# A forgetting-attention bias added by matmul instead of by rows read back from memory

## What is computed

```python
def fox_prompt(q, k, v, logf):
    ft = jnp.swapaxes(jnp.cumsum(logf, axis=1), 1, 2)
    for blk in range(s_len // Q_BLOCK):          # 2 blocks of 128 queries
        q0 = blk * Q_BLOCK
        kend = q0 + Q_BLOCK
        sc = jnp.einsum('bqhd,bkhd->bhqk', q[:, q0:kend], k[:, :kend]) * scale
        bias = ft[:, :, q0:kend, None] - ft[:, :, None, :kend]
        mask = jnp.arange(kend)[None, :] <= (q0 + jnp.arange(Q_BLOCK))[:, None]
        p = jax.nn.softmax(jnp.where(mask, sc + bias, -jnp.inf), axis=-1)
        ...
```

## Time and profile before

| | us |
|---|---|
| median of 3 runs | 1481.11 |
| lowest, highest | 1472.64, 1483.24 |
| time of the profiled execution | 1481.11 |
| its span, from first to last instruction | 1479.1 |

### The profile page before, as it was taken

The page is one execution under the profiler, slowest core; times in us unless marked ns, Lnnn a source line. Parts: engine busy times, 40 slices in busy tenths (PEclk is TensorE's granted clock), DMA queues, the critical chain, the costliest instruction groups (busy, mean ns, idle before and its releaser), DMA issues.

```text
span 1479.1 us, 15869 instructions
## 1 busy us (share of the span) xinstructions
PE 1383.4 (94%) x6315; PEld 630.3 (43%) x6315; DVE 343.9 (23%) x699; ACT 231.9 (16%) x461; POOL 25.5 (2%) x55
## 2 busy tenths in 40 slices
PE   6899899999978999999999999999999999999996
PEld 2555536666446434434334344333343333433332
DVE  3441322434243211101201121021011110120113
ACT  2011410433243211101101011011010010110102
POOL 1100000001000100000000000000000000000000
PEclk9799989999987799999999999999999999999998
DMA  8655347443145679999999999999999999999992
GB/s 292 207 199 182 139 170 257 138 163 108 71 171 187 279 284 419 429 428 426 430 425 428 427 421 427 428 427 427 422 427 428 428 418 408 427 428 427 427 429 107
DMA packets 72476, 486.83 MB, mean 329 GB/s; under 512 B 10349, under 2 KB 15205, under 8 KB 47828
## 3 DMA queue, kind: packets, MB, share of 16 engines
q1 hardware_dynamic: 70724, 480.85, 79.4%
q0 software_dynamic: 1680, 4.91, 1.0%
HBM read 481.63 MB, written 4.12 MB: 328 GB/s over the span
## 4 chain that ended last, share of the span: by engine, by line
PE 76%; DMA 17%; DVE 2%; issue 2%; ACT 2%; SPq 1%; DVEq 0%; ACTq 0%; PEldq 0%
PE bank L1726 35%; DMA ring<-in_w_gate_up_dram 16%; PE bank L1373 9%; PE bank L1691 5%; PE bank L1400 4%; PE bank L1265 4%; PE bank L1714 3%; PE bank L1692 3%; PE bank L1560 2%; PE bank L1356 2%; PE bank L1517 1%; PE bank L1368 1%; PE bank L1355 1%; PE bank L1628 1%; PE bank L1646 1%
## 5 line engine op out<-in xcount | busy, mean ns | idle before, releaser
L1726 PE MATMUL bank<-ring,work 128*64 128x512 f32 x2048 | 457.2, 600 | 16.7 <-issue 10.8
L1726 PEld LDWEIGHTS bank<-ring,work 128*64 128x64 f32 x2048 | 161.1, 138 | 291.0 <-issue 290.8
L1726 PE MATMUL bank<-ring,hT 128*64 128x512 f32 x1024 | 233.3, 603 | 16.6 <-DMA ring<-in_w_gate_up_dram 16.6
L1242 DVE TENSOR_TENSOR gbT<-gbT,bank 128x512 f32<-128x512 f32 x85 | 58.4, 688 | 452.8 <-PE bank L1714 392.2
L1373 PE MATMUL bank<-hT,ring 128*128 128x320 f32 x512 | 143.4, 440 | 5.6 <-DVEq L805 4.9
L1726 PEld LDWEIGHTS bank<-ring,hT 128*64 128x64 f32 x1024 | 77.0, 138 | 161.5 <-issue 161.5
L1373 PEld LDWEIGHTS bank<-hT,ring 128*128 128x128 f32 x512 | 97.7, 193 | 53.5 <-issue 7.0
L1211 DVE TENSOR_SCALAR work<-bank 128x512 f32<-128x512 f32 x32 | 22.0, 686 | 322.8 <-PE bank L1726 322.8
L1400 PE MATMUL bank<-hT,ring 128*128 128x320 f32 x256 | 72.4, 436 | 0.0
L1691 PE MATMUL bank<-qT,tok 128*128 128x256 f32 x256 | 72.4, 405 | 0.0
L707 ACT ACTIVATE work<-bank 128x320 f32<-128x320 f32 x16 | 7.0, 438 | 408.4 <-PE bank L1265 408.4
(11 more groups left out here) (334 smaller groups left out, 894.2 us busy)
## 6 DMA issues: line engine op xcount, KB each, us to landing
ring<-in_w_gate_up_dram SPq DMA_DIRECT2D x128, 2048.0 KB, 14.8
ring<-in_w_down_dram SPq DMA_DIRECT2D x64, 2048.0 KB, 17.0
ring<-in_w_ada_dram SPq DMA_DIRECT2D x12, 2048.0 KB, 8.1
ring<-in_w_in_dram SPq DMA_DIRECT2D x12, 2048.0 KB, 9.8
ring<-in_cache_k_dram SPq DMA_DIRECT2D x16, 512.0 KB, 6.1
ring<-in_cache_v_dram SPq DMA_DIRECT2D x16, 512.0 KB, 4.5
ring<-in_w_out_dram SPq DMA_DIRECT2D x2, 2048.0 KB, 7.9
out_dram<-tok POOLq DMA_DIRECT2D x2, 1024.0 KB, 5.2
```

What stands on the lines that cost most here:

```text
L1242: TTo(piece(gbf, n), piece(gbf, n), B[6 + n % 2][:, :], ALU.add).then_inc(s["scatter_read"], 1)
L1726: last = mm(bank[CAP * x:CAP * x + CAP, :], lhsT[:, CAP * x:CAP * x + CAP], rhs(x), start=start, stop=stop)
```

## The change

The bias and the mask no longer meet in `biasF`. The write to and the six reads from `bias_rows`, `masked`, and the semaphores `bias_out`, `bias_in` and `bias_made` are gone. DVE adds the mask itself to the scores at L917. PE adds the bias row: after each two scores matmuls, which now leave the sum open (`stop=False`), it adds two matmuls of 16 rows, whose weights are one column of the identity, repeated 128 times, and whose moving operand is `Fp`. A one in row h of the weights picks row h of `Fp` for all 128 queries. For a pair of heads these are two of 128 columns and two of 256. `scores_ps` is raised by the last of a head's matmuls. PE waits for `F_made` ahead of `scores(0)`. On SyncE's queue chunks 7 to 21 stand together, and the wait for `rg_free` stands ahead of the first cached keys.

```diff
-            for c in range(7, 20):
+            for c in range(7, 22):
                 chunk(c)
-            eng.wait_ge(s["F_made"], 1)
-            eng.dma_start(bias_d, Fp).then_inc(s["bias_out"], 16)
-            chunk(20)
-            eng.wait_ge(s["rg_free"], 1)
-            eng.wait_ge(s["bias_out"], 16)
-            bias_rows(0, 8)
-            chunk(21)
...
             chunk(22)
-            eng.wait_ge(s["scores_read"], 4)
-            bias_rows(8, 12)
             chunk(23)
-            eng.wait_ge(s["scores_read"], 8)
-            eng.wait_ge(s["bias_made"], 2)
-            bias_rows(12, 16)
+            eng.wait_ge(s["rg_free"], 1)
             keys_in(0)
...
-            def masked(a, z):
-                eng.wait_ge(s["bias_in"], 32 * (1, 2, 3)[(z - 8) // 4])
-                v = biasF[:, a % 8:a % 8 + z - a, :].rearrange("p s (t n) -> p s t n", t=3)
-                for t in (0, 2):
-                    link.later(TTo(v[:, :, t, :], v[:, :, t, :], mask[:, 0:128].unsqueeze(1).to_broadcast([128, z - a, 128]), ALU.add))
-                eng.wait_ge(s["chain_dve"], link.n)
-                eng.sem_inc(s["bias_made"], 1)
-
...
-                TTo(P, B[h % 4][:, 0:384], biasF[:, h % 8, :], ALU.add).then_inc(s["scores_read"], 1)
+                TTo(P, B[h % 4][:, 0:384], mask, ALU.add).then_inc(s["scores_read"], 1)
...
-                        last = mm(B[2 * (p % 2) + o][:, c:c + n], qT[d, p, q:q + 128], kT[d, p, 0:n], start=True, stop=True)
+                        mm(B[2 * (p % 2) + o][:, c:c + n], qT[d, p, q:q + 128], kT[d, p, 0:n], start=True, stop=False)
+                    for o in range(2):
+                        row = ident[0:H, 2 * p + o:2 * p + o + 1].to_broadcast([H, 128])
+                        last = mm(B[2 * (p % 2) + o][:, c:c + n], row, Fp[:, 0:n], start=False, stop=True)
                         if c:
                             last.then_inc(s["scores_ps"], 1)
...
+            eng.wait_ge(s["F_made"], 1)
             scores(0)
             scores(1)
```

More of the change, by code:

```diff
@@ L126, in hybrid_layer @@
         U = Uf.rearrange("p (t c) -> p t c", t=NT)
-        biasF = work[:, 0:3072].rearrange("p (s n) -> p s n", s=8)
         Ssb = work[:, 3072:4608].rearrange("p (s n) -> p s n", s=4)
@@ L251, in hybrid_layer @@
             den_made mult_made st_made rg_done F_made
-            bias_out bias_in bias_made scores_ps scores_read negmax_made exp_done probs_made PT_ps PT_ev py_ps py_read
+            scores_ps scores_read negmax_made exp_done probs_made PT_ps PT_ev py_ps py_read
             qbd_zero qbd_made KT_ps KT_ev sscores_ps sscores_read snegmax_made sexp_done sprobs_made
@@ L295, in hybrid_layer @@
         G_K, G_LF, G_V, G_ST, G_CF = 0, 6, 7, 13, 15
-        bias_d = nc.dram_tensor("bias_rows", (H, SP_), f32, kind="Internal").ap()
         block = ctx.enter_context(nc.Block())
@@ L341, in chunk @@
                 eng.dma_start(wstage[c % 3], CHUNKS[c]).then_inc(chunk_in[c % 3], 16)
[L343 to L347, removed]
             for c in range(7):
@@ L938, in gated @@
                 link(STT(v, v, 1.0, windows(U, S0, DS)[:, t, :, :], ALU.add, ALU.mult))
-            masked(0, 8)
             for h in range(4):
@@ L945, in _ @@
                 head_norm(2 * p + 1)
-                if p in (2, 4):
-                    masked(4 * p // 2 + 4, 4 * p // 2 + 8)
                 if p + 2 < NT:
```

## The result

| | before | changed |
|---|---|---|
| median, us | 1480.14 (1472.64 to 1483.24, 4 runs) | 1499.64 (1498.5 to 1501.39, 4 runs) |
| profiled execution: time, span | 1481.11, 1479.1 | 1496.86, 1495.1 |

The changed kernel is slower: the ratio to the kernel before is 1.015 (95% interval 1.0126 to 1.0174), 19.5 us between the medians. A ratio here is not the quotient of two medians, which would be 1.013; a ratio of 1.015 stands for 22 us. I had forecast 11.9 us, and within 1% as the likeliest class.

A forecast was written before the change was run, and what follows sets the result against it. PE was taken to bound the prompt's attention, with shifts there reaching the end. Added matmuls of 12.6 us less a vanished wait of 0.7 gave 11.9 us, on 1481.1 us a forecast of 1493.0 us, range 1483 to 1502.

The forecast's parts named there:

- within 1%: Whole kernel's time: a change of less than one per cent, 14.8 us, either way; chance 0.67.
- That PE bounds the stretch, and that a shift there reaches the end whole: Prompt's attention, 263.8 to 360.2 us: PE busy 94.46 of 96.40 us; any shift before 518 us moves the end equally.
- DVE, DMA and queue parts at 0: Removed additions of 5.0 us on DVE, about 3 MB of bias rows and queue waits: counted as 0 gain.
- 2 us earlier and not 4: SyncE's queue: first cached keys issued some 4 us earlier than at 295.93, with no effect.
- The wait at 270.63 gone: PE's wait of 0.73 us for L927, first turned probabilities of head 0, disappears: -0.7 us.
- The added matmuls at 1.58 us a pair: Scores in the prompt's attention: 2 x 0.25 + 2 x 0.54 us a pair, 12.6 us for eight pairs.
- rival A: Scores blocks: three extra changes of shape a pair at 0.30 us each, 16.8 us, 1498 us; chance 0.19.
- The clock: Prompt's attention, 263.8 to 360.2 us: granted clock 1.00 in the profile; the sum had no term for a fall there.
- Rival B: From 410 to 520 us: shifted clock falls give back half of 24 us lost, 1481 us or less; chance 0.09.
- Rival D: Scores blocks: the two heads' additions share the array, 6.3 less 0.7 is 5.6 us, 1487 us; chance 0.09.

The follow-up runs named there:

- e1: Changed kernel without the added matmuls, so the scores lack the forget bias: 1481.74 us, ratio 0.9994 to the kernel before.
- e6: Changed kernel with the two heads' additions side by side in different halves of the array, 16 rows for each head: 1492.61 us, ratio 1.0078.
- e7: Changed kernel with each 16-row matmul preceded by a second of the same shape with zero weights: 1521.4 us, ratio 1.0289.
- e3: Changed kernel with a pair's four additions grouped ahead of its four scores matmuls: 1497.63 us, ratio 1.0087.
- e8: Changed kernel with a pair's four additions grouped ahead of its scores, and 128 rows in each instead of 16: 1495.29 us, ratio 1.0107.
- e4: Changed kernel with 128 rows instead of 16 in the added matmuls: 1494.78 us, ratio 1.0074.
- e5: Changed kernel with the two heads' additions side by side in different halves of the array, 64 rows each: 1487.95 us, ratio 1.0044.
- e11: Kernel before with 46 idle matmuls in PE's waits in the samples' attention and 30 more at about 173 us: 1472.33 us, ratio 0.9922.

## Why the prediction was wrong

*That PE bounds the stretch, and that a shift there reaches the end whole:* right. The stretch grew by 19.3 us, the samples' and the experts' parts by -0.2 and -0.8.

*DVE, DMA and queue parts at 0:* right (e1: stretch 96.76 in both). The keys were issued at 293.85 against 295.93, 2 us earlier and not 4, with no effect.

*The wait at 270.63 gone:* right, and a little more. From the first gate projection to the next block it was 10.42 us before (265.33 to 275.75), and 9.46 in e6 (267.62 to 277.08), which has no fall there and the changed kernel's shapes around it: 0.96 us back instead of 0.73.

*The added matmuls at 1.58 us a pair:* here a term was mis-sized. I had each matmul right as a stream (0.22 and 0.43 us by e7) and put 0.29 us a pair on top by taking 0.25 and 0.54. But the additions bring three more changes of shape to a pair, at 0.19 to 0.20 us each (e3, e6), 0.60 us. A pair costs 1.89 us, eight cost 15.1 instead of 12.6. The price stood in the trace of the kernel before, and I misread it: I took the 0.20 us that the old block has above its columns for the whole of two changes of shape, where half of their 0.40 us lies outside the block (344.47 to 349.20 above). L1494 did not show it either: it stands for one matmul of a kind, going in, while in e7 both the first and the last of a run take about 0.1 us more than the ones between. I had named rival A for this and given it 0.30 a change; the truth, 0.20, lay between forecast and rival.

*The clock:* here a step was missing. I took the stretch's clock of 1.00 as given for the changed one. Serial 16-row matmuls make it fall two or three times: 1.77 us in the first two blocks (7.25 against 2 x 2.74), 1.47 us in the gate projection at 268.74 (5.88 to the next start, where e6 takes 4.41) and 1.68 in the one at 322.91, 4.9 us in sum. e3 against e8, and the changed kernel against e4, differ in the rows of these matmuls and show it: falls with 16, none with 128. That rows decide is shown; how they do it is not. Rival B had the clock in it, but at another place and with a gain.

Sum: 15.1 + 4.9 - 0.96 = 19.0 us, against 19.3 in the stretch and 19.5 between the medians. The forecast was 12.6 - 0.7 = 11.9. *Rival D* (heads side by side) was rightly put aside for this layout, and e5 shows what it would take: the second head's rows on other partitions.

## What to carry to other kernels

Work moved from an idle engine to the one that bounds a stage costs its full price, however small; DVE and the queue had room here, PE had none. A small matmul among matmuls of another shape is to be counted as columns plus 0.2 us for each change of shape, going in and coming out; the same operands padded with rows of zeros to the neighbours' shape, and put side by side, cut the added block from 1.89 to 0.66 us. To read the price of a change of shape, compare the whole passage with and without the small matmuls: a part of it lies in the neighbours. And a clock of 1.00 in the kernel before is no property of the stage: with 16-row matmuls it fell for the unchanged matmuls around them, while idle matmuls with all 128 rows in PE's waits raised it and, in all, gave 0.8%.

## What the runs showed of the hardware that I had not expected

- The granted clock fell to the lower level with 16-row matmuls in the stream (0.96, 0.96, 0.95, 0.94 in four profiles, 0.92 with twice as many), once after 21 us in which PE had not waited at all; with 64 or 128 rows, or with the 16-row matmuls side by side in half the time, it stayed at 1.00 in four.
- Rows of zeros were free: two additions of 128 columns took 0.64 us with 128 rows and with 16.
- A change of shape, between 16, 64 and 128 rows alike, cost 0.20 to 0.22 us in seven kernels.
- Matmuls that compute nothing made the kernel faster where they stood in the place of a wait, also ahead of matmuls with 32 weight columns (L1356 before, L1360 in e11: eight in 1.07 us against 1.93).
